# Norms of 128x4 numbers laid out by SyncE, bias rows copied by GpSimd, and a changed order of operands, chunks and sigmoids in a decoder layer

## What is computed

```
def rms_norm(x, g):
    y = x32 * lax.rsqrt(jnp.mean(x32 * x32, axis=-1, keepdims=True) + EPS)
    return (y * g.astype(jnp.float32)).astype(x.dtype)

def swiglu(x, w_gate, w_up, w_down):
    return (jax.nn.silu(x @ w_gate) * (x @ w_up)) @ w_down
```

## Time and profile before

| | us |
|---|---|
| median of 3 runs | 2040.07 (2038.50 to 2041.54) |
| the profiled execution | 2038.7 |
| its span in the trace | 2036.9 |
| mean granted TensorE clock (1.0 is full) | 0.999 |

### The profile page before, as it was taken

The page is one execution under the profiler, slowest core; times in us unless marked ns, Lnnn a source line. Parts: engine busy times, 40 slices in busy tenths (PEclk is TensorE's granted clock), DMA queues, the critical chain, the costliest instruction groups (busy, mean ns, idle before and its releaser), DMA issues.

```text
span 2036.9 us, 26353 instructions
## 1 busy us (share of the span) xinstructions
PE 2010.5 (99%) x9374; PEld 1639.7 (80%) x9374; DVE 1362.1 (67%) x2333; ACT 784.0 (38%) x1479; POOL 83.5 (4%) x94
## 2 busy tenths in 40 slices
PE   8999999999999999999999999999999999999998
PEld 6878888888888877777777888888888888888886
DVE  7886666666988455555666443458876676667886
ACT  6342332334455343333455112135433333334453
POOL 1000000000012100100100000000000000000021
PEclk9999999999999999999999999999999999999999
DMA  5233333247444311101114111114233323267433
GB/s 186 78 112 127 124 126 108 98 171 280 159 125 150 109 33 48 37 32 42 43 62 144 53 53 47 47 50 150 95 113 109 101 101 109 78 227 252 142 96 126
DMA packets 97563, 221.23 MB, mean 109 GB/s; under 512 B 20159, under 2 KB 20195, under 8 KB 95648
## 3 DMA queue, kind: packets, MB, share of 16 engines
q1 hardware_dynamic: 69568, 164.66, 24.1%
q10 hardware_dynamic: 22800, 46.29, 6.6%
q0 software_dynamic: 5072, 8.68, 1.3%
HBM read 164.41 MB, written 59.08 MB: 110 GB/s over the span
## 4 chain that ended last, share of the span: by engine, by line
PE 94%; DVE 4%; ACT 1%; issue 1%; DMA 0%; DVEq 0%; ACTq 0%; SPq 0%
PE bank L2017 20%; PE bank L2018 20%; PE bank L2019 20%; PE bank L1953 10%; PE bank L1954 10%; PE bank L1955 10%; PE bank L2184 2%; PE bank L2221 1%; PE bank L2197 1%; DVE op_l L1386 0%; DVE B_l L1380 0%; DVE gs_l L1420 0%; PE bank L2234 0%; DMA h<-xT 0%; PE bank L1977 0%
## 5 line engine op out<-in xcount | busy, mean ns | idle before, releaser
L1953 PE MATMUL bank<-xh,wh 128*128 128x512 f32 x640 | 255.4, 399 | 0.0
L2017 PE MATMUL bank<-B_h,op_h 128*128 128x512 f32 x624 | 245.4, 393 | 9.3 <-DVE op_l L1386 9.0
L2017 PE MATMUL bank<-T_h,op_h 128*128 128x512 f32 x640 | 250.0, 391 | 1.9 <-DVE U L1477 1.9
L2018 PE MATMUL bank<-T_l,op_h 128*128 128x512 f32 x640 | 249.7, 390 | 0.0
L1954 PE MATMUL bank<-xl,wh 128*128 128x512 f32 x640 | 249.6, 390 | 0.0
L1955 PE MATMUL bank<-xh,wl 128*128 128x512 f32 x640 | 249.6, 390 | 0.0
L2019 PE MATMUL bank<-T_h,op_l 128*128 128x512 f32 x640 | 249.5, 390 | 0.0
L2019 PE MATMUL bank<-B_h,op_l 128*128 128x512 f32 x624 | 243.3, 390 | 0.0
L2018 PE MATMUL bank<-B_l,op_h 128*128 128x512 f32 x624 | 243.3, 390 | 0.0
L2017 PE MATMUL bank<-gs_h,op_h 128*128 128x512 f32 x616 | 240.5, 390 | 0.7 <-DVE gs_l L1420 0.7
L2019 PE MATMUL bank<-gs_h,op_l 128*128 128x512 f32 x616 | 239.7, 389 | 0.0
(11 more groups left out here) (211 smaller groups left out, 3379.8 us busy)
## 6 DMA issues: line engine op xcount, KB each, us to landing
gr<-g_ops SPq DMA_DIRECT2D x154, 256.0 KB, 2.7
raw<-stream SPq DMA_DIRECT2D x56, 512.0 KB, 3.5
gate<-ffn_in SPq DMA_DIRECT2D x44, 512.0 KB, 4.0
up<-ffn_in SPq DMA_DIRECT2D x44, 512.0 KB, 4.9
g_ops<-tT SPq DMA_DIRECT2D x78, 256.0 KB, 2.0
g_ops<-gb SPq DMA_DIRECT2D x58, 256.0 KB, 5.1
A<-ffn_down ACTq DMA_DIRECT2D x6, 1536.0 KB, 6.9
h_spill<-h ACTq DMA_DIRECT2D x32, 256.0 KB, 2.7
```

The source lines that it names most:

```text
L1953: nc.tensor.matmul(out, wh[slot][:, cols], hi, start=first, stop=False)
L2017: nc.tensor.matmul(out, op_h[slot][:, cols], hi, start=first, stop=False, skip_group_check=True)
L2018: nc.tensor.matmul(out, op_h[slot][:, cols], lo, start=False, stop=False, skip_group_check=True)
```

## The change

- **Norms 0 and 2.** `sum_squares` now makes four products with one moving column, so a token stands on its own partition, 128x4 numbers for a token half (`rstd_4`). `root_of` and the reciprocal (`invert_4`) work on these. SyncE writes the 512 numbers to HBM in 4-byte pieces (`rstd_tok`) and, once this has landed (`rstd_out`), reads them back as a row for all 128 partitions (`rstd_in`); `lay_out_rstd`. `rstd_4` holds one token half, so the second half's root waits for the first write. `SUM_AT`, `E_TIME`, `G_TIME` and the lists of steps change with that. `normalise` and `combine` are written earlier than before.
- **Bias rows.** GpSimd clears `rows` and fills it by 32 copies of runs (`distance_runs`) from a table transposed on the host, and one more for mixer B. The product, ScalarE's copies and the 198 KB are gone.
- **Start.** TensorE first makes 14 products of `ones` with `ones`. Operand 1 is split right after k 3. The second token half is split ahead of the first half's squares.
- **Moving data.** In the split for the pairs B22 comes ahead of B11 and B21.
- **Attention.** The split of a mixed half is the last item of its chunk's misc jobs. The last three chunks' pv use banks 7, 6, 7 in turn.
- **Merge.** The sigmoids of t = 0 and 1 are together at its head, that of t = 3 right behind that of t = 2.

The diff's core:

```diff
-X_READY = {"T2": 17, "T1": 19, "T3": 21, "T4": 23, "B11": 25, "B21": 27, "B22": 29}
+X_READY = {"T2": 17, "T1": 19, "T3": 21, "T4": 23, "B22": 25, "B11": 27, "B21": 29}
...
-E_TIME = (7, 13, 15, 19, 24, 27, 31, 31)
-G_TIME = (8, 14, 16, 20, 25, 28, 32, 35)
+E_TIME = (9, 12, 15, 19, 24, 27, 31, 31)
+G_TIME = (10, 13, 16, 20, 25, 28, 32, 35)
...
-            if (u, s) in Y_AT:
-                plan.append(("mix", "y", Y_AT[(u, s)]))
...
             plan += misc
             refill()
+            if (u, s) in Y_AT:
+                plan.append(("mix", "y", Y_AT[(u, s)]))
...
+def pv_bank(c):
+    return 7 if c in (CHUNKS - 3, CHUNKS - 1) else 6
...
-SUM_AT = ((5, 8), (7, 9))
-INVERT_AT = ((6, 9), (7, 9))
+SUM_AT = ((7, 10), (5, 8))
+ROOT_AT = 6
...
+            def lay_out_rstd(f, hf):
+                n = 2 * f + hf
+                sp_.wait_ge(rstd_4_made, n + 1)
+                sp_.dma_start(rstd_tok[n].rearrange("(c p) -> p c", p=P), rstd_4[:], allow_slow_non_contiguous=True).then_inc(rstd_out, 16)
+                sp_.wait_ge(rstd_out, 16 * (n + 1))
+                sp_.dma_start(rstd[:, hf * HALF:(hf + 1) * HALF], rstd_tok[n].partition_broadcast(P)).then_inc(rstd_in, 16)
...
                     load_up(f, p + 2)
+                    if p == 0:
+                        lay_out_rstd(f, 0)
+                        lay_out_rstd(f, 1)
...
-            pool.wait_ge(x_in[3], 16)
-            pool.dma_start(hot[:], onehot).then_inc(tab_in, 16)
+            nc.gpsimd.memset(rows[:], NEG).then_inc(rows_cleared, 1)
...
+            for v, first, n, b, step in runs:
+                values = tab[:, b:b + 1].to_broadcast([HEADS, n]) if step == 0 else tab[:, b:b + (n - 1) * step + 1:step]
+                nc.gpsimd.tensor_copy(rows[:, v, first:first + n], values).then_inc(rows_made, 1)
...
+                if norm % 2 == 0:
+                    if norm + hf:
+                        act.wait_ge(rstd_out, 16 * (norm + hf))
+                    nc.scalar.activation(rstd_4[:], bank[NORM_BANK[norm][hf]][:, 0:4], ACT.Sqrt, bias=eps[:, 0:1]).then_inc(root, 1)
+                    return
...
             for k in range(2, KT):
                 raw_low(0, 0, k)
-            for o in range(1, 4):
+                if k == 3:
+                    operand_low(0, 1)
+            for o in range(2, 4):
                 operand_low(0, o)
-            add_squares(0, 0)
             for k in range(KT):
                 raw_low(0, 1, k)
+            add_squares(0, 0)
...
+                if norm % 2 == 0:
+                    for c in range(4):
+                        last = nc.tensor.matmul(bank[NORM_BANK[norm][hf]][:, c:c + 1], acc[hf][:, c * P:(c + 1) * P], ones[:, 0:1], start=c == 0, stop=True,
...
+            pe.wait_ge(made, 2)
+            for _ in range(14):
+                nc.tensor.matmul(bank[7][:, 0:P], ones[:], ones[:], start=True, stop=True)
             ffn(0)
...
-                    if c:
+                    if c >= CHUNKS - 3:
+                        pe.wait_ge(pv_out, c - 1)
+                    elif c:
                         pe.wait_ge(pv_out, c)
...
+                if first_step:
+                    stored_sigmoids(0)
+                    stored_sigmoids(1)
```

The lists of `moving_low`, of which the last entries say most, before and after:

```diff
-                                                           (31, "B11", 0), (31, "B11", 1), (33, "B21", 0), (34, "B21", 1),
-                                                           (36, "B22", 0), (36, "B22", 1)):
+                                                           (30, "B22", 0), (31, "B22", 1), (32, "B11", 0), (32, "B11", 1),
+                                                           (34, "B21", 0), (35, "B21", 1)):
```

More of the change, by code:

```diff
@@ L1048, in ffn @@
                                 plain_silu(f, p, h_)
-                    for x, first in (("T2", 19), ("T1", 20), ("T3", 21), ("T4", 28), ("B11", 31), ("B21", 32), ("B22", 33)):
+                    for x, first in (("T2", 18), ("T1", 19), ("T3", 20), ("T4", 28), ("B22", 29), ("B11", 31), ("B21", 32)):
                         for part in range(2):
@@ L1848, in _ @@
                     kind, i, g = unit_of(u)
[L1849 removed]
+                    src = bank[pv_bank(c)][:, 0:2 * P]
                     dve.wait_ge(pv_done, c + 1)
@@ L2133, in ffn @@
                 for s in range(STEPS):
-                    if s == 4 and not f:
-                        distance_biases()
                     if s in SUM_AT[f]:
```

141 lines of the change are left out of this document (80 added, 61 removed).

## The result

| | before | after |
|---|---|---|
| median, us | 2039.93 (2038.50 to 2041.54, 4 runs) | 2054.62 (2053.48 to 2055.32, 4 runs) |
| ratio to before | | 1.0072, 95% interval 1.0060 to 1.0084 |
| profiled execution, span | 2038.7, 2036.9 | 2053.5, 2051.7 |

The account below looks back on a forecast made before the run. TensorE, busy 99% of the span, was taken as the bound. 6.3 - 2.6 - 0.1 + 1.9 + 1.0 = 6.5 us off the profiled 2038.7 gave 2032.2; with 1.4 for the median, 2033.6, range 2026.5 to 2038.0.

Parts of the forecast that it names:

- The start: First FFN's beginning: step 4 at 19.7 instead of 24.4, full clock behind it, sums 0.12 dearer; gain 6.3 us at step 32.
- the clock's gain: TensorE from 24.40 to 28.20, behind the distance product: clock 0.55 before, full speed expected after; 1.7 us won.
- the products of ones: 14 TensorE products before the real ones; if they don't raise the clock, 0.6 us lost at most.
- Attention: Mixed half's split last removes the og wait, gain 1.9 us; two banks for pv remove ybl's wait, gain 1.0.
- The new wait: First norms' trip through HBM: write 4.2 us, second half back at 45.3, 5.7 us of slack, price 0.
- the bound of 7.1: Upper bound for the norm write, in us, from statistics writes of 512 pieces in 8 KB; slack just none there.
- The read-back: Norm's return from HBM to all partitions, put at 3.0 us for the first half.
- the limit of 51: Latest time, in us, for the second half's norm numbers to be back before VectorE's work up to B11's split.
- the norms come late: Rival, chance 0.10: writes beyond 7.0 us lengthen each FFN's B11 stop by 2o - 14.1; at 12, 2053.4 us.
- B22 ahead of B11: Step 33, both FFNs: TensorE stops 2.8 us each, 5.8 with restarts; 3.2 saved on other waits; net loss 2.6.
- the clock rival: Rival, chance 0.10: the clock falls in the new B11 stops, twice 1.7 us, giving 2037.0 us.

Follow-up runs that it names:

- the attention run: Kernel before with only two edits, the mixed half's split last in its chunk and two banks for the last three pv: 2033.87 against 2039.98, ratio 0.9969.
- the run with 16-byte pieces: Changed kernel, norm written as 128 pieces of 16 bytes instead of 512 of 4, tokens wrongly paired: 2035.58 us against 2040.00, ratio 0.9982.
- the seven writes: Changed kernel plus seven small SyncE writes between first FFN and attention; 512 4-byte pieces took 9.5 us side by side, 2.0 when 64 bytes apart.
- old order of the splits: Changed kernel with splits of B11, B21 and B22 in the order of before, norms still through HBM: 2045.96 us against 2040.00, ratio 1.0026.

## Why the prediction was wrong

- **The start was right, in part by luck.** Step 4 was forecast at 19.7 and came at 19.66; the gain at step 10, with the sums, was 6.5 where 6.3 stood for the whole stage. The real products start 0.5 us later than assumed (8.33), because the 14 products of ones take 6.3 us and not 4.0 in this execution, and step 4 came on time even so. The 1.7 us booked as the clock's gain hold against the one profiled execution of before; the attention run shows that the distance product doesn't cost them each time. So part of this gain was luck of the execution. And the products of ones are worth 1.2 us at step 4, not 0.6.
- **Attention was right.** 3.0 us were won between the FFNs, 2.9 forecast; the run with these edits alone shows 3.1 on the trace. The og wait is 0.3, ybl's is replaced by 0.4 for pt.
- **The step that failed is "The new wait", "The price of this wait is 0".** The write was put at 4.2 us by taking a quarter of what four-number pieces took beyond a plain transfer, on the reading that those writes were slow because they shared the queue. It measured 8.3 and 9.0 us in the first FFN and 10.7 and 7.2 in the second; the bound of 7.1 was passed as well. The rows behind that bound were of another kind: the statistics go out four numbers at a time, so in pieces of 16 bytes, which the prediction's last sentence on this wait calls 4-byte pieces. The rule of the Trainium skill that was quoted there (DMA: Bandwidth & Descriptors, Rules for kernel authors), one descriptor per element, pointed the right way, against the write. The traces agree with it: queue q1 has 1536 packets more in the changed kernel (72256) than in the run with 16-byte pieces (70720), as four writes of 512 pieces have against four of 128. But the count isn't what made the write slow: 512 pieces of 16 bytes took 2.5 us alone, 512 of 4 bytes 64 bytes apart 2.0, and 128 of 4 bytes side by side 7.3.
- **The read-back was low too:** 3.0 forecast, 4.4 and 5.7 measured in the first FFN. With both, the second half's numbers were back at 56.5, not 45.3, and past the limit of 51.
- **The price of lateness was mis-sized.** The rival "the norms come late" named the mechanism and a place, and put the break-even at a write of 8.7 us, which is the median that came. With the measured writes (17.3 and 17.9 us for the two of an FFN) its formula gives stops in step 33 that are 3.2 and 3.8 us longer, so a kernel even with before. It missed the stop at step 18, where ScalarE's operand halves stand behind a silu that waits for a `t` that waits for the norm: 4.8 us. It held the clock apart as another rival, though both come with the same stops. And steps 32 to 39 grew by 5.5 and 4.7 us over the run with 16-byte pieces, more than the formula's, as the read-back was longer and as VectorE's lateness passes from `t` to ScalarE's silu, B_h and op_h and back to VectorE's op_l and B_l.
- **B22 ahead of B11 was right in kind, and the clock rival was right with it.** With the write short, the stop in step 33 was 2.85 us, 2.8 forecast. But each had a stretch at the lower clock behind it (0.58 and 0.61), so each cost 4.7 and not 2.9 (steps 32 and 33 take 10.15 us instead of 5.44). The forecast with the clock rival's 3.4 us on top was 2037.0; the run with 16-byte pieces, where only these two things are left, had 2035.6. The warning of the Trainium skill cited in that rival (TensorE: Matmul & The Clock Gate, Why this matters for your kernels), that idle gaps bring the lower level back, agrees with most rows here. In the traces of before, of the change and of the experiments but the seven writes, 16 of TensorE's 20 stops of over 2 us had the lower level in them or within 2 us behind them; those of 2.28, 2.33, 2.64 (og) and 3.34 us had not. Against the rival stood that the og pause of 2.6 us was followed by full pace; one row of that kind was no ground for 0.10.
- **Sum by the trace,** up to the last product of the second FFN: -6.5 start, -3.0 attention, +4.8 between steps 10 and 20, +8.9 and +8.2 from step 32 to step 40 of the two FFNs, +0.2 in the second FFN's sums: +12.6, as in the table. Of the 8.9 and 8.2, 3.5 each are there with the quick write too (table, 16-byte pieces: 26.9 us from step 32 to 40 against 23.4), so they are the order's and its clock's; the rest, 5.5 and 4.7, and the 4.8 are the late norm's. Another 2.2 us came after the last product, at the lower clock.

## What to carry to other kernels

When a small result takes a trip through HBM, its latency is set by how the pieces lie there, and must be measured in that pattern before slack is weighed against it; here one access pattern was worth 15 us on the trace. A late value is not priced at one reader: every engine's queue behind it has to be followed, here to ScalarE's operands behind a silu as well as to VectorE's splits. And a TensorE stop of over 2 us in this kernel was mostly paid twice: once as idle time, and once more in a slower clock, about 2 us on top of a stop of 2.8.

## What the runs showed of the hardware

- 4-byte pieces written side by side in HBM took 7.0 to 9.5 us for 128, 256 or 512 of them; the same 512 pieces 64 bytes apart took 2.0, 128 pieces of 16 bytes 2.0, 512 of 16 bytes 2.5.
- A stride between neighbouring float32 numbers in SBUF cost each engine that read or wrote with it: VectorE's 128x512 product 1.07 us instead of 0.69 (read, 16 bytes), ScalarE's square 1.14 instead of 0.62 (write, 512 bytes), TensorE's sum 1.80 instead of 0.95 (weights, 16 bytes).
- The same instructions at the same place had the lower clock level in one profiled execution and not in another (0.55 and 1.00 from 24.40 to 28.20; from a stop of 0.8 us on, between 1062 and 1071 us, in five traces of thirteen), and the times of the kernel before lie in steps of about 1.6 us.
- 16 of 20 TensorE stops of over 2 us had the lower level in them or right behind them, but not one of 3.34 us (clock 1.00 from 109.71 to 113.70, old order of the splits).
